# An output projection of four row-block products per tile as seven half-size products, with weight sums kept in DRAM

## The reference

```python
h = rms_norm(x, attn_norm)
q, k, v, f_logit, u, cv, cb, cc, g = split(h @ w_in)
y_a = forgetting_attention(q, k, v, f_logit, b_forget) @ w_proj_attn
y_b = multiscale_pool(u, pool_w, pool_scale) @ w_proj_pool
y_c = short_gated_conv(cv, cb, cc, conv_w) @ w_proj_conv
gates = sigmoid(g + b_gate)                    # three per channel
mixed = gates[0] * y_a + gates[1] * y_b + gates[2] * y_c
x = x + mixed @ w_out                          # 512x1024 @ 1024x1024: the output projection
h = rms_norm(x, ffn_norm)
a, b = split(h @ w_gate_up)
x = x + (silu(a) * b) @ w_down
out = rms_norm(x, final_norm)
```

## Time and profile before

| | us |
|---|---|
| median of 3 runs (lowest to highest) | 776.98 (776.23 to 777.86) |
| the profiled execution, its own time | 776.07 |
| its span, first to last instruction | 774.2 |
| PE busy in the span | 765.7 (99%) |
| DVE busy | 619.7 (80%) |
| ACT busy | 411.8 (53%) |
| mean granted TensorE clock | 0.999 of full |

### The profile page before, as it was taken

The page is one execution under the profiler, slowest core; times in us unless marked ns, Lnnn a source line. Parts: engine busy times, 40 slices in busy tenths (PEclk is TensorE's granted clock), DMA queues, the critical chain, the costliest instruction groups (busy, mean ns, idle before and its releaser), DMA issues.

```text
span 774.2 us, 12156 instructions
## 1 busy us (share of the span) xinstructions
PE 765.7 (99%) x4475; PEld 680.8 (88%) x4475; DVE 619.7 (80%) x1004; ACT 411.8 (53%) x702; POOL 18.3 (2%) x41
## 2 busy tenths in 40 slices
PE   8999999999999999999999999999999999999997
PEld 7888888888889999999988888999999998888885
DVE  6588777776898778776735699899999985799997
ACT  6536555756645555555434544555555552665554
POOL 2001100100000000000000000000000000000001
PEclk9999999999999999999999999999999999999999
DMA  5643242324234343334362523333333364353422
GB/s 192 176 110 83 56 108 57 83 55 109 55 82 110 98 121 84 107 92 127 111 216 82 164 90 100 110 105 111 95 103 109 110 192 162 125 174 121 148 99 110
DMA packets 127358, 87.92 MB, mean 114 GB/s; under 512 B 5612, under 2 KB 114212, under 8 KB 127300
## 3 DMA queue, kind: packets, MB, share of 16 engines
q1 hardware_dynamic: 126644, 86.82, 38.0%
q10 hardware_dynamic: 144, 0.26, 0.1%
q0 software_dynamic: 512, 0.07, 0.1%
HBM read 82.87 MB, written 4.19 MB: 112 GB/s over the span
## 4 chain that ended last, share of the span: by engine, by line
PE 98%; issue 0%; DMA 0%; ACT 0%; DVE 0%; POOL 0%; POOLq 0%; DVEq 0%
PE bank L831 10%; PE bank L835 10%; PE bank L833 10%; PE bank L1259 7%; PE bank L1261 7%; PE bank L1257 7%; PE bank L1070 4%; PE bank L1311 4%; PE bank L1313 4%; PE bank L1068 4%; PE bank L1312 4%; PE bank L1066 4%; PE bank L1104 2%; PE bank L1105 2%; PE bank L1106 2%; PE bank L1148 2%
## 5 line engine op out<-in xcount | busy, mean ns | idle before, releaser
L831 PE MATMUL bank<-operands,whi 128*128 128x512 f32 x352 | 138.1, 392 | 0.0
L835 PE MATMUL bank<-operands,wlo 128*128 128x512 f32 x352 | 137.3, 390 | 0.0
L833 PE MATMUL bank<-operands,whi 128*128 128x512 f32 x352 | 137.2, 390 | 0.0
L1973 DVE TENSOR_TENSOR wlo<-raw,whi 128x1024 fp32r<-128x1024 f32 x55 | 67.2, 1223 | 39.0 <-ACT whi L1377 38.3
L835 PEld LDWEIGHTS bank<-operands,wlo 128*128 128x128 f32 x352 | 66.1, 188 | 13.9
L833 PEld LDWEIGHTS bank<-operands,whi 128*128 128x128 f32 x352 | 66.2, 188 | 13.3
L831 PEld LDWEIGHTS bank<-operands,whi 128*128 128x128 f32 x352 | 66.1, 188 | 13.2
L1377 ACT CAST whi<-raw 128x1024 fp32r<-128x1024 f32 x55 | 57.7, 1050 | 33.9 <-PE bank L1152 21.0
L1261 PE MATMUL bank<-sums_hi,wlo 128*128 128x256 f32 x240 | 68.1, 284 | 0.0
L1259 PE MATMUL bank<-sums_lo,whi 128*128 128x256 f32 x240 | 68.0, 284 | 0.0
L1257 PE MATMUL bank<-sums_hi,whi 128*128 128x256 f32 x240 | 68.0, 284 | 0.0
(11 more groups left out here) (311 smaller groups left out, 1984.8 us busy)
## 6 DMA issues: line engine op xcount, KB each, us to landing
raw<-in_w_in_dram SPq DMA_DIRECT2D x105, 256.0 KB, 3.3
raw<-in_w_gate_up_dram SPq DMA_DIRECT2D x88, 256.0 KB, 3.3
raw<-in_w_down_dram SPq DMA_DIRECT2D x53, 256.0 KB, 2.9
big_x<-in_x_dram SPq DMA_DIRECT2D x8, 512.0 KB, 5.6
raw<-in_w_out_dram SPq DMA_DIRECT2D x16, 256.0 KB, 3.1
raw<-in_w_proj_attn_dram SPq DMA_DIRECT2D x8, 256.0 KB, 4.0
raw<-in_w_proj_pool_dram SPq DMA_DIRECT2D x8, 256.0 KB, 3.9
raw<-in_w_proj_conv_dram SPq DMA_DIRECT2D x8, 256.0 KB, 4.0
```

The lines of the kernel that those rows point to most:

```text
L831: nc.tensor.matmul(banks[b][:, 0:width], whi[:, s, w], op(hi + k * S), start=a, stop=False)
L833: nc.tensor.matmul(banks[b][:, 0:width], whi[:, s, w], op(lo + k * S), start=False, stop=False)
L835: mm = nc.tensor.matmul(banks[b][:, 0:width], wlo[:, s, w], op(hi + k * S), start=False, stop=z)
L1973: nc.vector.tensor_tensor(wlo[:, s, :], raw[:, s, :], whi[:, s, :].bitcast(F32), ALU.subtract).then_inc(w_lo, 1)
```

## The change

Two things are rearranged.

*The product.* For each pair of row blocks of `w_out` (even E, odd O, each with a left and a right half of 512 columns) and each pair of token blocks, the four quarter products of a 2x2 block product are formed from seven products of sums. `OUT_PARTS` is the order of their 28 steps (product, pair of row blocks), two steps to a unit, 14 units. Three products take the weights as they are; four take sums of them. The mixed rows of two channel blocks are kept as seven operands of 256 columns (`E1, O1, O2, M3, M1, M2, M4`), high and low.

*The sums of weights.* Four sums, each of all of a quarter of `w_out` (128x2048, 1 MB), are made early. Four loads bring the quarters into a part of `operands` that is not in use yet, VectorE adds (`out_sum(0)` to `out_sum(3)`), SyncE stores the results in DRAM (`keep_sums`), and the output stage loads them from there. ScalarE waits in pair 0 for all four stores.

```diff
--- before.py
+++ after.py
@@ -414,6 +414,46 @@
+        E1, O1, O2, M3, M1, M2, M4 = range(7)
+        MIX_COLS = 7 * S // 2
+        MIX_AT = [T0, T0 + 2 * MIX_COLS, T0 + 4 * MIX_COLS, BR[0][0]]
+
+        def mixed(i, slot, low, n=1):
+
+            at = MIX_AT[i] + low * MIX_COLS + slot * (S // 2)
+            return operands[:, at:at + n * (S // 2)]
+
+        def mixed_32(i, slot, n=1):
+
+            at = MIX_AT[i] + MIX_COLS + slot * (S // 2) - 2 * DB * S
+            return tiles_32[:, at:at + n * (S // 2)]
+
+        Q1, Q5, Q2_, Q6, Q3, Q7, Q4 = range(7)
+        OUT_PARTS = ([(Q1, 0), (Q1, 1), (Q5, 0), (Q5, 1), (Q2_, 0), (Q2_, 1), (Q1, 2), (Q5, 2),
+                      (Q1, 3), (Q5, 3), (Q2_, 2)] + [(Q6, i) for i in range(4)]
+                     + [(Q3, i) for i in range(4)] + [(Q7, i) for i in range(4)] + [(Q2_, 3)]
+                     + [(Q4, i) for i in range(4)])
+        OUT_AB, OUT_DB, OUT_EB = (0, 2), (1, 3), (4, 5)
+        OUT_BANKS = {Q1: (OUT_AB, 1), Q5: (OUT_DB, 1), Q2_: (OUT_EB, 1), Q6: (OUT_AB, 2),
+                     Q3: (OUT_DB, 2), Q7: (OUT_AB, 3), Q4: (OUT_AB, 4)}
+        OUT_ROWS = {Q1: E1, Q5: M1, Q2_: O1, Q6: M2, Q3: M4, Q7: M3, Q4: O2}
+        OUT_SUMS = {Q5: 0, Q7: 1, Q6: 2, Q4: 3}
...
+        def out_sums(kind):
+
+            at = (0, 2 * HALF * 2, 4 * WB * S, 4 * WB * S + 2 * HALF * 2)[kind]
+            return tiles_32[:, at:at + 4 * HALF]
...
@@ -601,15 +644,41 @@
             load_rows("front", 0, 2, w_in, 4 * P, COL_V // HALF)
             load_x(3)
 
+            def load_sums(kind):
+
+                e, c = ((0, 1), (0, 0), (1, 0), (1, 1))[kind]
+                src = w_out.rearrange("(r e p) c -> p r e c", e=2, p=P)
+                sp.dma_start(out_sums(kind).rearrange("p (r c) -> p r c", c=HALF),
+                             src[:, :, e, c * HALF:(c + 1) * HALF]).then_inc(sums_in[kind], 16)
+
+            def keep_sums(kind):
+
+                sp.wait_ge(out_summed, kind + 1)
+                dst = w_sums[4 * kind * P:4 * (kind + 1) * P, :].rearrange("(r p) c -> p r c", p=P)
+                sp.dma_start(dst, out_sums(kind).rearrange("p (r c) -> p r c", c=HALF)
+                             ).then_inc(sums_kept, 16)
+
+            load_sums(0)
+            load_sums(1)
+
             wait_full(sp, 3, "norm", 0, 2)
             sp.dma_start(pw_raw.rearrange("p (g d) -> p g d", g=4),
                          pool_w[0].rearrange("g c d -> c g d")).then_inc(pool_w_in, 16)
             load_rows("front", 0, 3, w_in, 6 * P, COL_V // HALF)
             for j, col in enumerate([COL_U + g * P for g in range(4)] + [COL_F]):
                 load("front", 0, VALUE_UNITS + j, columns(w_in, col))
+                if j in (1, 3):
+                    load_sums(2 + j // 2)
+            keep_sums(0)
             for i in range(WB):
                 for j, col in enumerate((COL_Q, COL_K, COL_CV, COL_CB, COL_CC)):
                     load("pair", i, j, columns(w_in, i * P + col))
+                    if i == 0 and j == 0:
+                        keep_sums(1)
+                    elif i == 0 and j == 4:
+                        keep_sums(2)
+                    elif i == 1 and j == 0:
+                        keep_sums(3)
 
             def gate_columns(br, block):
                 return columns(w_in, COL_G + br * D + block * P)
...
+            sp.wait_ge(sums_kept, 64)
+            for j in range(14):
+                if j == SLOTS:
+                if j in (SLOTS, SLOTS + 1):
+                    for t in range(2 * (j - SLOTS), 2 * (j - SLOTS) + 2):
                         sp.dma_start(big_x[:, t * D:(t + 1) * D], x[t * P:(t + 1) * P, :]
                                      ).then_inc(x_again, 16)
-                load_rows("out", 0, j, w_out, j % 4 * 2 * P, j // 4)
+                load("out", 0, j, [(out_part(*part), at)
+                                   for at, part in enumerate(OUT_PARTS[2 * j:2 * j + 2])], HALF)
...
+            def out_product(n):
+
+                part, i = OUT_PARTS[n]
+                (pair, k), s = OUT_BANKS[part], unit("out", 0, n // 2)[1]
+                pe.wait_ge(mix_lo, i + 1)
+                w = slice(n % 2 * HALF, (n % 2 + 1) * HALF)
+                onto = part in (Q6, Q3, Q7, Q4)
+                for m in range(2):
+                    to = banks[pair[m]][:]
+                    if i == 0:
+                        begin(pair[m], "out", 0, k)
+                        if part == Q5 and m == 1:
+                            pe.wait_ge(y_free, 2 * len(ROUNDS) - 1)
+                    h, l = [mixed(i, OUT_ROWS[part], low)[:, m * P:(m + 1) * P] for low in (0, 1)]
+                    nc.tensor.matmul(to, h, whi[:, s, w], start=i == 0 and not onto, stop=False,
+                                     skip_group_check=onto)
+                    nc.tensor.matmul(to, h, wlo[:, s, w], start=False, stop=False,
+                                     skip_group_check=onto)
+                    mm = nc.tensor.matmul(to, l, whi[:, s, w], start=False, stop=i == 3,
+                                          skip_group_check=onto)
+                    if i == 3 and (m == 0 or n % 2 == 0):
+                        mm.then_inc(full[pair[m]], 1)
+                return mm
...
+            for j in range(14):
+                unit_ready("out", 0, j)
...
@@ -1522,6 +1599,8 @@
                     wait_full(act, b, "pair", i, k)
                     nc.scalar.copy(wk(PV_LO, S, half_rows(a)), banks[b][half_rows(1 - a), :]
                                    ).then_inc(v_lo_part, 1)
+                if i == 0:
+                    act.wait_ge(sums_kept, 64)
                 for a, b, k in ((0, 7, 1), (1, 3, 5)):
                     rows = half_rows(a)
                     wait_free(act, b, "pair", i, k)
...
-            def merged_hi(r, m):
-
-                act.wait_ge(merged, merged_by(r) + 1 + m)
-                operand_hi(op(MX_HI + (2 * ROUNDS[r][0] + m) * S), wk(ACC + m))
+            def mixed_hi(r):
+
+                i = ROUNDS[r][0]
+                act.wait_ge(merged, merged_by(r) + 2)
+                pair = work[:, ACC * S:(ACC + 2) * S].rearrange("p (m c) -> p m c", m=2)
+                nc.scalar.copy(mixed(i, E1, 0, 2).rearrange("p (m c) -> p m c", m=2),
+                               pair[:, :, 0:TOK])
...
@@ -2049,8 +2135,20 @@
             normed(3)
             for k in range(DB):
                 token_low(k, 1)
+            def out_sum(kind):
+
+                to, a, b = ((0, 0, 1), (1, 1, 2), (2, 0, 2), (3, 2, 3))[kind]
+                for k in {a, b}:
+                    dve.wait_ge(sums_in[k], 16)
+                if kind:
+                    dve.wait_ge(out_summed, kind)
+                nc.vector.tensor_tensor(out_sums(to), out_sums(a), out_sums(b), ALU.add
+                                        ).then_inc(out_summed, 1)
+
+            out_sum(0)
             for j in range(3, 6):
                 split_lo("front", 0, j)
+            out_sum(1)
             for t in range(TB):
                 dve.wait_ge(values_hi, t + 1)
                 nc.vector.tensor_tensor(value_parts(t, True), value_rows(t),
@@ -2152,6 +2250,8 @@
                                                   op(KK[a], S, rows).bitcast(F32), ALU.subtract)
                 ins.then_inc(free[1], 1)
                 split_lo("pair", i, 4)
+                if i == 0:
+                    out_sum(2)
 
                 for a in range(2):
                     lg = big_y[:, a * L_COLS:(a + 1) * L_COLS]
@@ -2180,6 +2280,8 @@
                     ins.then_inc(probs, 1)
                     if a == 0:
                         split_lo("pair", i, 5)
+                    elif i == 0:
+                        out_sum(3)
                 for a in range(2):
                     for j in range(TB):
                         operand_lo("pair", i, 4 + 4 * a + j,
...
@@ -2320,12 +2422,35 @@
-                               op(MX_LO + at), wk(ACC + m))
+            def mix_sums(r):
+
+                i = ROUNDS[r][0]
+                dve.wait_ge(merged, merged_by(r) + 2)
+                both = work[:, ACC * S:(ACC + 2) * S]
+                e1, e2, o1, o2 = [both[:, q * TOK:(q + 1) * TOK] for q in range(4)]
+                step(nc.vector.tensor_tensor(
+                    pair_of(mixed_32(i, M3, 2)), pair_of(both)[:, 0:4:3, :],
+                    e2.unsqueeze(1).to_broadcast([P, 2, TOK]), ALU.subtract))
+                step(nc.vector.scalar_tensor_tensor(
+                    out=mixed_32(i, M2), in0=mixed_32(i, M1), scalar=-1.0, in1=e1,
+                    op0=ALU.mult, op1=ALU.subtract))
+                nc.vector.scalar_tensor_tensor(
+                    out=mixed_32(i, M4), in0=o1, scalar=-1.0, in1=mixed_32(i, M2),
+                    op0=ALU.mult, op1=ALU.subtract).then_inc(mix_summed, 1)
+
+            def mixed_lo(r):
+
+                i = ROUNDS[r][0]
+                dve.wait_ge(mix_hi, i + 1)
```

(52 more changed lines are left out.)

226 lines of the change are left out of this document (102 added, 124 removed).

## The result

The changed kernel takes 784.36 us (median of 4 runs, 783.75 to 784.66) where the kernel before, run beside it, took 776.72 (4 runs, 776.23 to 777.86): ratio 1.0095, 95% interval 1.0078 to 1.0113. It is slower by 7.6 us. The forecast was 784.0.

What follows compares the result with a forecast made beforehand. TensorE, busy in 99% of the span, was taken to bound the kernel. Terms: -5.4 + 1.8 + 8.4 + 2.2 = +7.0, 783.1 on the profiled 776.07, plus 0.9 to the median: 784.0 us; range 778.5 to 788.

Steps and rivals of the forecast that it cites:

- The gain: Output stage: 168 steps of matmuls on TensorE instead of 192, 24 x 0.227 = 5.4 us less.
- Stalls of the output stage: TensorE waits for VectorE's remainders: 1.0 us at units 2 and 3, 0.8 at unit 14; 1.8 us, bounds 0 and 5.
- Case (d): Output stage starves because units load too late into three slots, 3 us more: 787; chance 0.1.
- Front stage: Loads and sums 0 and 1 fit into idle DMA time and VectorE's gaps: cost 0; without cover 2.3 us each.
- Rounds: Some 2.2 us more VectorE work in rounds 1, 4 and 7, covered by slack: cost 0; without cover up to 2.2 each.
- Pair 0: Sum 2 delays the logits, late loads of units 14 and 15 the second value product: 8.4 us, bounds 4.7 and 10.8.
- X: Pair 0: time from a sum's end to landing of the unit behind its store; 6.5 us, bounds 4.3 and 7.7.
- the first term: Pair 0: sum 2 ahead of the first head's row maxima makes TensorE 2.2 us late at the second head's logits.
- The clock: After 6.2 us standing still in pair 0, TensorE runs slower for a while: +2.2 us, bounds 0 and 3.5.
- case (b): The clock stays at 2.4 GHz after pair 0's gap: 781.8 us; chance 0.25.
- (c): Pair 0: stores do not hold up loads, 4.7 us late, no clock drop: +1.1, 778.1 us; chance 0.08.
- (e): Faster: unit 15 in time in pair 0 through a short landing; limit 775.6, or 773.8 with clean output stage; chance 0.07.

Runs made afterwards that it cites:

- e7: e8 with VectorE's and ScalarE's work on output units 2, 3 and 14 moved earlier in their order; 770.99 us, ratio 0.9927.
- e5: Changed kernel with the output stage alone: no early loads, sums or stores, plain weights read in place of the sums; 773.25 us, ratio 0.9952.
- e8: Changed kernel with sum 2 moved to the front stage, store 2 behind unit 9's load, store 3 behind unit 15's; 773.27 us, ratio 0.9953.
- e1: Changed kernel with stores 2 and 3 behind the loads of units 14 and 15 in SyncE's queue; 776.24 us, ratio 0.9994.
- e9: Changed kernel with stores 2 and 3 sent twice, 2 MB ahead of each load; 791.84 us, ratio 1.0188.
- e10: Changed kernel with stores 2 and 3 issued by GpSimd in its own queue; 775.74 us, ratio 0.9996.
- e3: Changed kernel with 44 transposes on TensorE into an idle bank ahead of pair 0's second value product; 782.61 us, ratio 1.0071.
- e4: Changed kernel with stores 2 and 3 cut to 8 KB, waits kept, output stage reading plain weights; 777.9 us, ratio 1.0017.
- e2: Changed kernel with sums 2 and 3 in the front stage, their stores behind the loads of units 9 and 10; 775.25 us, ratio 0.9979.
- e6: Kernel before plus only the change's early loads, sums, stores and ScalarE's wait, the sums read by nobody; 787.63 us, ratio 1.0138.

## Why the prediction was right

**The gain (-5.4)** is shown whole by e7, where the stage lasts from 390.42 to 430.3 = 39.9 us instead of 45.3.

**Stalls of the output stage (+1.8; measured +2.15).** In the kernel after, the stage begins at 400.1; these matmuls end the waits at its units 2 and 3 and at the unit behind its end (timeline of TensorE):

```profile
406.18 0.50 PE L1247 MATMUL bank<-whi,operands 128*128 128x512 f32 x1 [0.41 <-DVE wlo L2059]
...
409.46 0.50 PE L1247 MATMUL bank<-whi,operands 128*128 128x512 f32 x1 [0.27 <-DVE wlo L2059]
...
442.11 0.50 PE L911 MATMUL bank<-operands,whi 128*128 128x512 f32 x1 [0.67 <-DVE wlo L2059]
```

They are the three that the prediction named, 0.41 + 0.27 at the head and 0.67 at the end. The first matmul behind each wait lasts 0.50 instead of 0.39, and the next starts 0.33 behind it instead of 0.23; with that 1.7, and with the slower hand-over ahead of them 2.15. The stage takes 42.0 us instead of 45.3: -3.3 net where -3.6 was predicted. e5's -3.2 by time and e7's 2.3 below e8 say the same. Case (d), starving, did not come: no other unit is waited for.

**Front stage (0).** Right. The loads landed where the DMA engines had been idle, and no gap opened. TensorE reaches pair 0's logits 0.41 us later than before, 0.38 of it already at its first weight matmul; e1 and e8 do not have this, so it is counted to the start and not to the change.

**Rounds (0).** Right. The output stage starts at 400.1 instead of 388.6, 11.5 us late, and the first quarter of the rounds was late by 11.55 at its own start already.

**Pair 0 (+8.4; measured +9.2).** The second value product starts at 104.58 instead of 94.96, 9.6 us late, 0.4 of it from the start. Every link but one is as worked out: sum 2 lasts 2.28 us; from the cast of unit 14 to sum 3 are 91.75 - 87.07 = 4.7 (4.8 predicted); from the cast of unit 15 to the product 3.5 (3.6). The link that was off is X, 6.5 predicted and 7.0 measured, twice in the sum. The transfer was put together from rates of 358 to 400 GB/s. What moved in the kernel after between 80.5 and 87 us, in 40 slices of 0.16 us (busy tenths of the DMA engines, and GB/s), shows where it fell short:

```profile
DMA  0007999999999999979989998999999999710000
GB/s 0 0 0 290 403 391 391 378 353 302 378 403 391 328 328 290 189 139 239 277 214 265 227 227 215 309 287 321 325 325 337 353 353 344 141 35 22 16 0 0
```

Adding up the slices from the left, the store's 1.05 MB end in the stretch of 139 to 277 GB/s, and the unit's 0.52 MB are the stretch of about 320 behind it. The packets in the trace say the same, as the store's have 2 KB and the load's 512 bytes: the store's lie between 81.0 and 84.6 us, its first three quarters at 380, 360 and 308 GB/s and its last at 227, with the DMA engines nearly as busy. The whole store takes some 0.6 us more than at 360. That is the missing half microsecond. Over e9's 2.1 MB there is one such stretch as well, 196 to 256 GB/s at the end of its second store.

A store's end is not slow by itself. In e1 the same store 2 has no load right behind it, and store 3 has. Windows of the end of store 2 in the kernel after, then of stores 2 and 3 in e1:

```profile
83.00:84.40 1.40, 1.40 (x8) 1.14 (x7) 0.95 (x5) 1.40 (x6) 1.40 (x3) 1.00 0.97 227
```

```profile
82.00:83.20 1.20, 1.20 (x7) 0.98 (x6) 1.20 (x5) 1.20 (x6) 0.73 (x2) 1.00 1.02 381
...
94.50:96.00 1.50, 1.50 (x8) 1.24 (x8) 1.38 (x3) 0.91 (x4) 0.00 (x0) 1.00 0.95 201
```

With nothing right behind it store 2 keeps 381 GB/s to its end; with loads right behind, its end falls to 227 and store 3's to 201. So a load queued right behind the store goes with the slow end, and without one it is gone. By what means was not tried.

The waits are split otherwise than predicted too: 1.4 at the logits, 0.8 at the transposes of the probabilities and 5.8 before the product, in place of 2.2 and 6.2. At the logits, the eight matmuls behind the wait are paced by the row maxima, 82.47 - 80.46 = 2.0 us instead of 79.86 - 78.50 = 1.36; the block behind them starts at 82.47, 2.6 us later than before and 2.2 without the 0.4 of the start, so the first term is as predicted after all.

By the fit in the Trainium skill (DMA: Bandwidth & Descriptors, "Anatomy of one DMA") a transfer of 1 MB takes an estimated 4.4 us. The section gives the fit for DMAs that GpSimd issues, and the prediction set it beside SyncE's without saying so. The two stores that GpSimd issues in e10 took 4.8 us; SyncE's four took 4.9 to 9.4, 6.3 in the median, so the measured row decides, as the prediction took it.

**The clock (+2.2; measured 1.8 to 1.9).** The lateness grows from 9.6 at the product to 11.55 at the rounds; e3 gives 1.75 of it back. The prediction took the size from the first transposes of the kernel, 0.22 us apart instead of 0.11, though it read the record of the granted clock as showing no lower value there. That reading was wrong: the trace of the kernel before has no entry of the clock until 8.03 us, behind these transposes, and the views show 1.00 where there is no entry. In e7's trace the first entry is at 11.70 us, and the slow transposes go on until then. So the record was no evidence for case (b). In the gap of pair 0 the record does show the fall to 0.50. The Trainium skill (TensorE: Matmul & The Clock Gate, "Part 1: The HAM clock gate") has the clock of an idle TensorE halved and given back after activity; by that rule, the trace agrees, at 0.50 and 1.00. With case (b), no fall, the time would have been near e3's 782.6.

**The sum.** -5.4 + 2.15 + 9.2 + 1.9 + 0.4 = +8.2 in the profiled execution, whose span grew by 8.3. The forecast of +7.0 came out 0.4 from the median only because the profiled execution of the kernel before lay 0.9 below its median and that of the changed kernel 0.2 above its own: that closeness is luck. Mechanism and place are as predicted; two terms were small by 0.8 and 0.35, one was large by 0.3, and the start's 0.4 stood in no term.

**The rivals.** (c), stores that don't hold up loads, would have had X at 4.3; e4, with hardly a byte in them, has 4.4, and e1 and e10 show what is left when nothing stands behind them. (e), faster, wanted X under 4.1, and no run with a load behind such a store had that. But its limit, 775.6, is near what e1 and e10 measure (776.24 and 775.74), and its 773.8 with a clean output stage is not far from e8's 773.27.

## What to carry to other kernels

An issue that waits for a computation holds up every load behind it in its queue, by the lateness of the computation and by the bytes of the transfer: when a store is added, look at what is queued behind it and who is next to want that, and put it behind those loads or in another queue. Extra work on an engine with 17 to 20% of slack still has to go where the slack is: the same four sums make the output stage start 0.1, 1.7 or 2.2 us late by their place alone (388.7, 390.3 and 390.8 us in the traces of e8, e2 and e1, against 388.6). When TensorE stands still it can cost more than the length of the wait, here 1.9 us on top of 5.8.

## What the runs showed of the hardware

- **The clock can fall after a short wait too.** In e4's profiled execution TensorE stood still for 2.1 us only before the second value product, and from 101.67 on the matmuls of 128x512 last 0.59 to 0.63 us, with the clock at 0.71 in the window and 0.86 in the next:

```profile
96.00:100.00 4.00, 2.17 (x12) 1.71 (x10) 1.63 (x5) 2.94 (x6) 0.00 (x0) 1.00 1.01 262
100.00:104.00 4.00, 3.69 (x14) 3.15 (x15) 3.83 (x6) 1.83 (x3) 0.00 (x0) 0.71 0.22 43
104.00:108.00 4.00, 4.00 (x16) 3.20 (x16) 3.39 (x6) 0.41 (x1) 0.00 (x0) 0.86 0.38 92
```

  The value product behind this wait, from 100.31 on, still ran at the full pace, and the fall came after it. That execution took 780.04 us, 2.1 above the median of its kernel. The other runs have no trace, but a mean clock: the four that took 779.05 us and more are all at 0.997, and six of the seven that took 778.39 and less are at 0.998 or 0.999. A wait of 1.4 us, at the logits, was followed by a fall in the traces of e3 and e6 and by none in those of the kernel after, e1, e4, e9 and e10. Case (c) counted on no drop of the clock after 2.5 us of standing still; these traces speak against that.
- **A store's last part is slow where a load is queued right behind it**, 201 and 227 GB/s against 381 where none is, as shown above.
- **The start of a kernel varies and its clock record begins late.** The first entry is at 8.03 us in the kernel before and at 11.70 in e7's trace; ahead of it only the durations tell the pace.
- **The three waits at the output stage have a slow first matmul behind them**, 0.50 us for 128x512 instead of 0.39 at the full clock, some 0.1 us each that the list of waits does not count. The first one behind a block of transposes, with no wait, is slow as well: 0.48 at 92.36 us in the kernel after.
